# Order of the S5 filter products on TensorE: eight full-array products first, then 64-row products from alternating partition halves

## The reference, cut to what matters

```
h   = scan of (abar * h + bbar @ u)                      # 32 groups, 64 states, 1024 steps
y   = einsum(h_re, c_re) - einsum(h_im, c_im) + d * u
out = gelu(y) * sigmoid(gelu(y) @ glu_w + glu_b)         # within a group
h1  = x + concat(y_rg, y_s5) @ w_out
```

## Time and profile before

| | |
|---|---|
| time, median of 3 runs | 2253.53 us (2251.64 to 2256.22) |
| profiled execution, span from first to last instruction | 2253.7 us |
| TensorE busy in it | 2157.0 us (96%) |
| VectorE, ScalarE, GpSimd busy | 1619.9, 1271.3, 458.0 us |
| mean granted TensorE clock | 0.983 |

### The profile page before, as it was taken

How to read it: one execution, slowest core, us unless ns; L and a number is a source line. 1 busy time by engine, 2 the same in 40 slices (tenths; PEclk the granted TensorE clock), 3 DMA queues, 4 the chain that set the end, 5 groups by cost and what they waited for, 6 DMA issues and landing times.

```text
span 2253.7 us, 32977 instructions
## 1 busy us (share of the span) xinstructions
PE 2157.0 (96%) x9642; PEld 1693.2 (75%) x9643; DVE 1619.9 (72%) x1572; ACT 1271.3 (56%) x1213; POOL 458.0 (20%) x357
## 2 busy tenths in 40 slices
PE   7999999999996899999999999999999999999996
PEld 4454877887785688887787888788878787887873
DVE  5645743405537899787879977997889779997793
ACT  3135342514313577666667756775677667775673
POOL 0792000000000122122231222321322122222210
PEclk9999999999997899999999999999999999999997
DMA  5102332111233799899899979998999799997895
GB/s 174 38 1 96 105 131 83 38 38 38 68 129 110 295 377 374 302 329 310 283 316 375 377 270 317 377 375 309 325 327 363 271 319 372 378 378 269 306 344 174
DMA packets 233653, 555.72 MB, mean 247 GB/s; under 512 B 19972, under 2 KB 20200, under 8 KB 232392
## 3 DMA queue, kind: packets, MB, share of 16 engines
q1 hardware_dynamic: 218448, 512.41, 62.0%
q0 software_dynamic: 13200, 42.37, 7.5%
q10 hardware_dynamic: 1960, 0.35, 0.1%
HBM read 518.12 MB, written 33.69 MB: 245 GB/s over the span
## 4 chain that ended last, share of the span: by engine, by line
PE 80%; issue 8%; DVE 6%; ACT 3%; DVEq 1%; DMA 1%; ACTq 1%; POOLq 0%
PE PS L984 21%; PE PS L648 20%; PE PS L988 11%; PE PS L1005 9%; PE PS L1012 5%; PE PS L806 4%; PE PS L846 4%; DVE WL L1940 2%; PE PS L976 2%; PE PS L1037 1%; ACT WH L1344 1%; PE PS L942 1%; PE PS L666 1%; PE PS L1065 1%; ACT WH L1367 1%
## 5 line engine op out<-in xcount | busy, mean ns | idle before, releaser
L1940 DVE TENSOR_TENSOR WL<-WA,WH 128x2048 fp32r<-128x2048 f32 x288 | 651.5, 2284 | 69.7 <-ACT WH L1367 48.8
L1940 DVE TENSOR_TENSOR WL<-H,WH 128x2048 fp32r<-128x2048 f32 x144 | 329.2, 2286 | 84.0 <-ACT WH L1344 63.5
L984 PE MATMUL PS<-WH,XEH 128*128 128x512 f32 x1344 | 362.5, 392 | 3.4 <-DVE WL L1940 3.4
L988 PE MATMUL PS<-WL,XEH 128*128 128x512 f32 x1344 | 352.1, 390 | 0.0
L1367 ACT CAST WH<-WA 128x2048 fp32r<-128x2048 f32 x140 | 267.2, 1910 | 146.1 <-PE PS L1012 145.3
L984 PE MATMUL PS<-WH,XEL 128*128 128x512 f32 x1152 | 310.3, 391 | 0.0
L984 PEld LDWEIGHTS PS<-WH,XEH 128*128 128x128 f32 x1344 | 253.5, 189 | 55.3 <-DVE WL L1940 3.8
L988 PEld LDWEIGHTS PS<-WL,XEH 128*128 128x128 f32 x1344 | 252.9, 188 | 52.9
L984 PEld LDWEIGHTS PS<-WH,XEL 128*128 128x128 f32 x1152 | 217.8, 189 | 46.2
L1005 PE MATMUL PS<-WH,HTH 128*128 128x512 f32 x672 | 187.6, 401 | 4.6 <-DVE HTL L2040 4.6
L1344 ACT CAST WH<-H 128x2048 fp32r<-128x2048 f32 x72 | 136.9, 1909 | 89.9 <-PE PS L988 87.3
(11 more groups left out here) (333 smaller groups left out, 2915.3 us busy)
## 6 DMA issues: line engine op xcount, KB each, us to landing
WA<-in_exp_w_gu SPq DMA_DIRECT2D x216, 1024.0 KB, 7.4
H<-in_exp_w_gu SPq DMA_DIRECT2D x72, 1024.0 KB, 6.5
WA<-in_exp_w_down SPq DMA_DIRECT2D x72, 1024.0 KB, 9.0
H<-in_exp_w_down SPq DMA_DIRECT2D x72, 1024.0 KB, 8.0
WB<-in_xa_wkv SPq DMA_DIRECT2D x4, 2048.0 KB, 7.9
WB<-in_w_in SPq DMA_DIRECT2D x3, 2048.0 KB, 9.5
y_acc<-H SPq DMA_DIRECT2D x9, 512.0 KB, 2.6
H<-in_x SPq DMA_DIRECT2D x4, 1024.0 KB, 6.0
```

Source lines behind the costliest of these rows:

```text
L984: nc.tensor.matmul(PS[:, 2 * h + t, :], x[:, KT4 * half + k, t * P:(t + 1) * P], WH[:, j % 4, k * HALF:(k + 1) * HALF], start=False, stop= ...
L988: ins = nc.tensor.matmul(PS[:, 2 * h + t, :], XEH[:, KT4 * half + k, t * P:(t + 1) * P], WL[:, j % 4, k * HALF:(k + 1) * HALF], start=Fals ...
L1940: v.tensor_tensor(WL[:, s, :], src, WH[:, s, :].bitcast(F32), sub).then_inc(done, 1)
```

## The change

The order of TensorE's products in the eight y units, the order of ScalarE's work around them, and the engine of one pair of casts.

On TensorE the full-array product of all 32 groups comes first, with only the first group of each bank opening the accumulation; then, pair of units by pair, the 64-row products, the even group's and the odd group's in turn, into two different banks. The waits for the states (`hp_done`) and for FM (`f_done`) now stand ahead of each pair's 64-row products and no longer ahead of its first full-array product. ScalarE casts the RG-LRU half ahead of all eight copies. The two casts of w_out's first half go to VectorE, ahead of the low parts, and increment the same semaphore `w_high`.

```diff
-            for n in range(8):
+            def y_groups(n):
+                return [8 * (n // 2) + 2 * j + n % 2 for j in range(4)]
+
+            for n in range(8):
+                o = begin(("y", n))
+                for j, g in enumerate(y_groups(n)):
+                    nc.tensor.matmul(o[:, j * P:(j + 1) * P], UT[:, g, :], MM[:, :, g * SC:(g + 1) * SC],
+                                     start=j == 0, stop=False, skip_group_check=True)
+            for n in range(0, 8, 2):
                 pe.wait_ge(hp_done, n // 2 + 1)
                 pe.wait_ge(f_done, n // 4 + 1)
-                o = begin(("y", n))
                 for j in range(4):
-                    g = 8 * (n // 2) + 2 * j + n % 2
-                    r = slice(NS * (g % 2), NS * (g % 2) + NS)
-                    oo = o[:, j * P:(j + 1) * P]
-                    mm(oo, UT[:, g, :], MM[:, :, g * SC:(g + 1) * SC], 0, 3)
                     for w2 in range(2):
-                        ins = mm(oo, HPV[r, w2, g // 2, :],
-                                 FM[r, w2, g // 2, :, :].rearrange("p a b -> p (a b)"), w2 + 1, 3)
-                end(("y", n), ins)
+                        for b in range(2):
+                            g = y_groups(n + b)[j]
+                            r = slice(NS * b, NS * b + NS)
+                            ins = nc.tensor.matmul(bank(("y", n + b))[:, j * P:(j + 1) * P], HPV[r, w2, g // 2, :],
+                                                   FM[r, w2, g // 2, :, :].rearrange("p a b -> p (a b)"),
+                                                   start=False, stop=j == 3 and w2 == 1, skip_group_check=True)
+                            if j == 3 and w2 == 1:
+                                end(("y", n + b), ins)
...
+            act.wait_ge(hp_done, 4)
+            for ct in range(CT):
+                nc.scalar.copy(y_high(ct), YT[:, ct, :]).then_inc(t_high, 1)
             for n in range(8):
-                if n == 2:
-                    act.wait_ge(hp_done, 4)
-                    for ct in range(CT):
-                        nc.scalar.copy(y_high(ct), YT[:, ct, :]).then_inc(t_high, 1)
-                if n == 4:
-                    o1_split_high(0)
                 u = ("y", n)
...
+            dve.wait_ge(hp_done, 4)
+            dve.wait_ge(w_in_s[chunk_no[("o1", 0)] % 2], 16 * (chunk_no[("o1", 0)] // 2 + 1))
+            for part in range(2):
+                ks = slice(4 * part, 4 * part + 4)
+                v.tensor_copy(o1_high(0)[:, ks, :], wslot(("o1", 0))[:, ks, :]).then_inc(w_high, 1)
             for ct in range(CT):
                 dve.wait_ge(t_high, ct + 1)
```

## The result

| | before | after |
|---|---|---|
| time, median (lowest to highest) | 2253.53 us (2251.64 to 2257.78) | 2235.64 us (2234.24 to 2237.39) |
| ratio of the times | | 0.9916, 95% interval 0.9904 to 0.9928 |
| span of the profiled execution | 2253.7 us | 2232.5 us |
| TensorE busy | 2157.0 us | 2135.6 us |
| mean granted TensorE clock | 0.983 | 0.984 |

What follows compares the result with a forecast made beforehand. TensorE, busy 96% of the span, was taken as the bound. 19.3 us saved in the y units less 0.5 for a copy gives 18.8: 2253.7 to 2234.9, or 2234.7 against the median; range 2231 to 2244.

Steps and rivals of the forecast that it cites:

- Full-array products, pitch 0.11: TensorE's y units: 64 full-array matmuls grouped first, 63 steps of 0.11 us, the last starting at 299.1 us.
- The seam of 0.20 us: TensorE's y units before: each switch between full-array and 64-row matmuls costs 0.20 us more than a 0.11 us step.
- 64-row products, pitch 0.0546, from the column halves: TensorE's y units: alternating row halves run side by side, 127 steps taking 6.9 us; TensorE through 19.3 us earlier.
- The kin row: Profile row of the state-input products: 64 matmuls alternating between column halves in 3.71 us, taken as model for row halves.
- both rivals on the halves: Row halves don't overlap: 2241.7 us, chance 0.18; each half change is a seam: 2254.3 or 2263.7 us, chance 0.04 each.
- the estimate from it, 0.071: 64-row matmuls: pitch from the skill page's 77% of ideal for four row tiles, 2.1 us later, at 2236.8 us.
- The reason given with that term: Why 0.0546 us was chosen for 64-row matmuls: only the state-input products alternate halves, there too in runs of two.
- States never waited for: TensorE's 64-row matmuls: last `hp_done` step at 297.06 us, wanted by the fourth block only at 304.7.
- ScalarE, one copy more at the tail: End of the y units: two units fill together, so one extra copy adds 0.5 us before the transposes.
- VectorE's casts: Two w_out casts, 1.25 us each, at worst 2.25; VectorE's work stays hidden with at least 4.5 us cover.
- No fall of the clock: TensorE's denser order keeps its clock; the rival, gain partly given back at half clock, about 2240 us, had chance 0.04.
- The shift reaches the end: From transposes to kernel end: nothing on the path has its own time, so all 18.8 us arrive, giving 2234.9 us.

## Why the prediction was right

- *Full-array products, pitch 0.11*: measured 0.11, 7.3 us. The seam of 0.20 us, read out of the distances between loads, is confirmed by the run that puts 30 of them back: 5.9 us of distance more, 6.0 by the term. (The prediction counts 64 seams before; 63 lie between the first y product and the last. Its sum does not use the count.)
- *64-row products, pitch 0.0546, from the column halves*: measured 0.0563, 7.42 us for the 7.2 forecast. That is 0.2 us. The kin row was the right end of the range, and the longer the run of one half, the nearer the other end (0.11) comes. No seam stands at any of the 63 changes of half, so both rivals on the halves fall. The Trainium skill ("TensorE: Matmul & The Clock Gate", Part 3) measured 3.07 times for four row tiles; the estimate from it, 0.071, was further off than the row, and nothing like a 77% limit shows with two tiles. The Trainium skill ("TensorEngine Tiling (Array Packing)", Key Properties) names a drain for a change of mode and not for a change of tile; the trace agrees, 0.20 us for the one and nothing for the other.
- *The reason given with that term* was loose. It rested on the kin having runs of two as well, and the account of why runs matter that I put to the test next was wrong: runs of four overlap as completely, eight partly, sixteen little. That the order chosen was short enough was, in this respect, luck.
- *States never waited for*: the fourth block starts near 298.2 + 96 x 0.056 = 303.6, the last state is ready at 295.8.
- *ScalarE, one copy more at the tail*: 1.07 us for two copies, as counted. *VectorE's casts*: 2.36 us for two, 2.5 forecast.
- *No fall of the clock*: the granted clock is 1.00 through the new order, as forecast.
- *The shift reaches the end*: 18.64 us in the stretch, 17.9 in the medians, and no row of the chain from the transposes to 375 us changed its duration. The 0.9 between median and forecast is smaller than the scatter the clock makes; it is the stretch, and not the median, that confirms the size.
- *What was priced too lightly*: the moved casts were written down as hidden, and their cover given as 4.5 us for VectorE. That they were also needed, 4.9 us and 1.9 for the clock, stood nowhere in the text, though the same rows gave it.

## What to carry to other kernels

Look at the starts of TensorE's weight loads, not at its busy share: where products of different array shape take turns, each turn costs 0.20 us here, and sorting them by shape cost nothing, with all eight banks free to be opened at once. Then let products that contract over half the rows go to the two row halves in turn, in runs of at most four matmuls (two float32 products), each half into a bank of its own; that halved their pitch here, from 0.11 to 0.056 us. No run here sends both halves to one bank, so whether that would do is open. When the matrix engine's stretch shrinks, ask in the same breath which engine now ends last, and move its work before it does, since the idle time made by it can cost clock on top (1.9 us here).

## What was not expected of the hardware

TensorE overlaps the two halves beyond strict program order: 128 matmuls took 7.4 us in runs of two, 7.5 in runs of four, 9.5 in runs of eight and 12.2 in runs of sixteen. Where runs are long, three steps are saved at each change of half, and three matmuls of the other half start ahead of their turn. And two weight loads of 128 columns, 188 ns each, start within 7 ns of each other when they go to different row halves.
